# Carrying the odd layer's recurrence inside its chunk stage, with arrays turned in the features stage

## Chip, cores and metric

One core of a Trainium2 chip. The metric is device time in microseconds of one execution of the whole kernel, as the median over runs. "The profiled execution" is one further execution with the hardware profiler.

## What is computed

The kernel runs two transformer blocks over 512 latent and 256 context tokens, width 1024, all in float32. The first block has an attention layer and then an odd layer. One half of the odd layer's mixer is a gated delta rule (RWKV-7), run forwards and backwards for eight heads of 64, first over the context tokens and then, from the state left there, over the latent ones:

```python
def step(S, inp):
    w_t, k_t, v_t, kk_t, a_t = inp[:5]
    sa = jnp.einsum('bhvk,bhk->bhv', S, kk_t)
    S = (S * w_t[:, :, None, :] - sa[..., None] * (kk_t * a_t)[:, :, None, :]
         + v_t[..., None] * k_t[:, :, None, :])
    return S, (jnp.einsum('bhvk,bhk->bhv', S, inp[5]) if emit else None)
```

The outputs y of both directions over the latent tokens are needed, and of the context only the final state.

## The kernel before

Every part is a stage of its own: `stage` (L31) opens a block in which each engine runs its own instruction list, ordered by semaphores alone, and ends with a barrier over all engines. Engines are named PE (TensorE), DVE (VectorE), ACT (ScalarE), POOL (GpSimd) and SP (SyncE, which here only issues DMAs). `steps_of` (L91) unrolls two steps and runs the rest as a loop of two. The 768 tokens (context first) are cut into NCH = 12 chunks of CH = 64; CC = 4 of them are context. Three stages carry the recurrence.

**rwkv_features (L1431)** loops over four tiles m of 128 feature rows by 768 tokens. SP loads r, k, v and small weights of tile m, and the modulation weights of a later layer (`wbuf`, 3 MB twice per tile), which `modulate` multiplies beside (L1546). PE makes the gate products X and Y (L1558, L1561) for both directions, the head norms Z (L1566), the output gate (L1570) and the bonus sum (L1576). ACT takes sigmoids, square root and exponents, DVE the scan of the decays (L1605), the reciprocal (L1596) and the products alpha, beta, kappa, rho (L1624 to L1627). POOL stores those feature-major to `rwkv_arrays`. Tile m+1 starts when the bonus of m (`tail_ready`) is done.

**rwkv_chunks (L1668)** treats each chunk by itself, both directions d at once. SP's `load` (L1731) brings nine tiles with feature rows on the partitions; load(i) waits until chunk i-2 has ended, and PE reads them at the start of chunk i. PE multiplies in 64x64 corners, `each` (L1758) being eight products for the four head pairs (16 records in the trace). One chunk is: keys with alpha and rho (`kar`), turns of beta and kappa, betas with alpha and rho (`bar`), turns of alpha, v and z, masks times v (`mv`), five levels of doubling in which z and x are updated (lx by PE, copied by ACT, then two products each for x and z, added by DVE), then au and the results g, f, h, y. DVE masks the results of `kar` and `bar`; POOL makes the level masks `lev` (L1940) and stores the four results to `rwkv_ch` (L1947).

**rwkv_recurrence (L1955)** reads these back and carries the state over the 12 chunks: state = (g . state + h) * w, y = state . f + y, with four rounds PE to DVE per chunk, and stores ys. The readout stage follows. Another scan, **gla_chunks (L2257)**, in the second block, is not changed; it carries its state inside its chunk loop and loads with `kqr` tiles of 64 partitions and `vf` tiles of 128.

## Time and profile before

| | us |
|---|---|
| runs | 5564.84, 5576.18, 5569.65 |
| median | 5569.65 |
| profiled execution | 5565.43 |
| its span, first to last instruction | 5563.8 |
| TensorE / VectorE / ScalarE busy | 4503.7 / 2522.7 / 1470.3 |

The views group instructions by source line, engine and tile: output tile, an arrow, input tiles. In a timeline "x16" is how many records were merged, and the bracket is the engine's idle time ahead with what ended it; "issue" there is idle time that no wait of the profile explains, or a wait on a semaphore that it does not show. TensorE's clock has two levels, 1.2 GHz (0.50) and 2.4 GHz (1.00); a granted clock between them is a mean over both. One matmul in float32 is two records.

### The profile page before, as it was taken

To read this page: it belongs to the slowest core of one execution; us is meant where nothing else is said; L and a number is where in the kernel's file an instruction comes from. 1 tells how busy PE (TensorE), PEld (TensorE's weight loads), DVE (VectorE), ACT (ScalarE), POOL (GpSimd) and SP (SyncE) were. 2 spreads that over 40 slices of the span, in tenths; PEclk is the share of its full clock that TensorE was granted. 3 is DMA by queue.
4 is the path that set the end of the run, shared out by engine and by line. 5 is a ranking of instruction groups with operands and counts; after the bars stand their busy time and mean duration, and the time that the engine had idled before them with its cause. 6 is when DMAs were issued, how large, how long until landed. Compare 5 with 4: busy or idle time off the path is not lost. (4 is left out here: it accounts for less than half of the span.)

```text
span 5563.8 us, 87721 instructions
## 1 busy us (share of the span) xinstructions
PE 4503.7 (81%) x35800; PEld 3791.5 (68%) x35800; DVE 2522.7 (45%) x3576; ACT 1470.3 (26%) x2457; POOL 585.6 (11%) x789
## 2 busy tenths in 40 slices
PE   7567799999885587757996949389999995656998
PEld 7444588888742477745995838278888883435997
DVE  3454443336356444435444232343335845764444
ACT  2144321123243111102222221222213322333222
POOL 2011100001011211211001000010001112320000
PEclk7788899999996799978998955599999996668999
DMA  3355322213467312143332322222222333342332
GB/s 126 100 174 174 127 63 67 65 57 92 132 218 261 107 51 57 53 138 104 93 94 64 100 82 55 75 95 69 59 65 65 106 117 119 117 155 81 96 95 72
DMA packets 671562, 561.57 MB, mean 101 GB/s; under 512 B 114269, under 2 KB 582433, under 8 KB 671232
## 3 DMA queue, kind: packets, MB, share of 16 engines
q1 hardware_dynamic: 639552, 453.54, 27.1%
q0 software_dynamic: 31680, 103.21, 5.1%
q8 instruction: 258, 4.23, 0.3%
q14 instruction: 72, 0.59, 0.0%
HBM read 459.96 MB, written 96.69 MB: 100 GB/s over the span
## 5 line engine op out<-in xcount | busy, mean ns | idle before, releaser
L86 PE MATMUL acc<-h_hi,w_hi 128*128 128x258 f32 (+2 forms) x4416 | 1402.3, 318 | 45.8 <-DVE h_lo L455 39.2
L88 PE MATMUL acc<-h_hi,w_lo 128*128 128x258 f32 (+2 forms) x4416 | 1398.7, 317 | 0.0
L87 PE MATMUL acc<-h_lo,w_hi 128*128 128x258 f32 (+2 forms) x4416 | 1397.2, 316 | 0.0
L86 PEld LDWEIGHTS acc<-h_hi,w_hi 128*128 128x128 f32 x4416 | 833.0, 189 | 113.1 <-DVE h_lo L455 22.8
L87 PEld LDWEIGHTS acc<-h_lo,w_hi 128*128 128x128 f32 x4416 | 833.9, 189 | 60.5 <-issue 0.5
L88 PEld LDWEIGHTS acc<-h_hi,w_lo 128*128 128x128 f32 x4416 | 833.4, 189 | 59.0
L334 ACT CAST w_hi<-staged 128x1024 fp32r<-128x1024 f32 (+1 forms) x414 | 406.9, 1028 | 576.2 <-PE acc L88 391.0
L442 DVE TENSOR_TENSOR w_lo<-staged,w_hi 128x1024 fp32r<-128x1024 f32 (+1 forms) x414 | 480.5, 1200 | 139.8 <-ACT w_hi L334 137.0
L86 PE MATMUL acc<-hidden_hi,w_hi 128*128 128x512 f32 (+1 forms) x1200 | 419.3, 349 | 66.9 <-DVE hidden_lo L573 66.9
L483 DVE COPY offset<-acc 128x2 f32<-128x2 f32 x276 | 43.7, 158 | 928.9 <-PE acc L88 926.1
L87 PE MATMUL acc<-hidden_lo,w_hi 128*128 128x512 f32 (+1 forms) x1200 | 418.9, 349 | 0.0
L88 PE MATMUL acc<-hidden_hi,w_lo 128*128 128x512 f32 (+1 forms) x1200 | 418.0, 348 | 0.0
L86 PEld LDWEIGHTS acc<-hidden_hi,w_hi 128*128 128x128 f32 x1200 | 228.8, 191 | 98.1 <-issue 68.8
L88 PEld LDWEIGHTS acc<-hidden_hi,w_lo 128*128 128x128 f32 x1200 | 228.5, 190 | 29.2
L87 PEld LDWEIGHTS acc<-hidden_lo,w_hi 128*128 128x128 f32 x1200 | 228.7, 191 | 28.5
L598 POOL COPY squares<-square 128x768 f32<-128x768 f32 (+1 forms) x8 | 6.4, 797 | 1717.8 <-ACT square L345 1717.8
L494 DVE SCALAR_TENSOR_TENSOR xT<-acc,modTsecond,xT 128x512 f32<-128x512 f32 x104 | 66.6, 666 | 256.6 <-PE acc L88 256.6
L388 ACT CAST hidden_hi<-up 128x768 f32 (+3 forms) x66 | 50.4, 763 | 487.3 <-DVE up L513 487.3
L2783 PEld LDWEIGHTS diag_ps<-xd,decay 128*128 128x128 f32 x512 | 94.6, 284 | 107.7 <-DVE decay L2907 107.6
L494 DVE SCALAR_TENSOR_TENSOR xT<-acc,modTfirst,xT 128x512 f32<-128x512 f32 x96 | 60.5, 658 | 233.3 <-PE acc L88 233.2
L384 ACT ACTIVATE gate<-gate,offset 128x512 f32<-128x512 f32 (+1 forms) x132 | 81.3, 647 | 319.7 <-DVE gate L484 319.7
L1160 PE MATMUL raw<-k_hi,q 128*128 128x512 f32 (+3 forms) x240 | 90.4, 382 | 88.6 <-DVE q L1255 85.4
(451 smaller groups left out, 7045.2 us busy)
## 6 DMA issues: line engine op xcount, KB each, us to landing
wmod<-in_mod_w SPq DMA_DIRECT2D x16, 3072.0 KB, 14.8
staged<-in_w_ffn_in SPq DMA_DIRECT2D x88, 512.0 KB, 4.6
staged<-in_ffn_w_in SPq DMA_DIRECT2D x88, 512.0 KB, 4.4
wmod<-in_w_mod SPq DMA_DIRECT2D x8, 3072.0 KB, 11.0
rows<-acum SPq DMA_DIRECT2D x48, 512.0 KB, 3.8
staged<-in_ssd_w_in SPq DMA_DIRECT2D x42, 512.0 KB, 4.6
wmod<-in_w_mod SPq DMA_DIRECT2D x8, 2048.0 KB, 8.2
proj<-gate POOLq DMA_DIRECT2D x40, 384.0 KB, 2.6
```

The lines of the kernel that those rows point to most:

```text
L86: nc.tensor.matmul(out, w[0], x[0], start=start, stop=False)
L87: nc.tensor.matmul(out, w[0], x[1], start=False, stop=False)
L88: return nc.tensor.matmul(out, w[1], x[0], start=False, stop=stop)
L334: nc.scalar.copy(ws[s].hi[:, 0:p.KT, cols], staged[:, 0:p.KT, cols]).then_inc(S["w_hi"], 1)
L384: op = nc.scalar.activation(gate[s][:, t0:t0 + tn], gate[s][:, t0:t0 + tn], ACT.Silu, bias=offset[s][0][:, b:b + 1])
L388: nc.scalar.copy(hidden.hi[:, bass.ds(i, 1), 0:TOK - lo], up[s][:, wide]).then_inc(S["hidden_hi"], 1)
L442: nc.vector.tensor_tensor(ws[s].lo[:, 0:p.KT, cols], staged[:, 0:p.KT, cols], ws[s].hi[:, 0:p.KT, cols].bitcast(F32), ALU.subtract).then_i ...
L483: nc.vector.tensor_copy(offset[s][j][:], a[:, 254:256])
L494: op = nc.vector.scalar_tensor_tensor(out=xt, in0=acc[2 * s + j][:, c0:c0 + tn], scalar=p.gates[:, bass.ds(2 * i + j, 1), b], in1=xt, op0= ...
L598: op = nc.gpsimd.tensor_copy(squares[:, wide], square[j][:, wide])
L1160: nc.tensor.matmul(b[:, c:c + size], q2[s][:, t.q0:t.q0 + P], k_hi[g % 2][:, key:key + size], start=True, stop=False)
L2783: mm = nc.tensor.matmul(diag_ps[d][:, h], decay[d][:, h], xd[d][:, h], start=True, stop=True)
```

## The change

The recurrence stage and the array `rwkv_ch` are gone. The chunk stage walks each direction in its own order (`order`), loads both feature-major and token-major arrays (24 DMAs per chunk, 8 of 128 partitions and 16 of 64), and carries the state in SBUF: per chunk two products with the state per direction (context chunks one), accumulated into the open sums. Context chunks leave out what only y needs. The part of the next chunk that needs no state, its "front" (kar, bar, the masks, the turn of z), is placed into the current chunk: one product set after the lx sets of each of levels 0 to 3, and the turn behind au. Level 4 leaves out the x product. PSUM gets two banks `front`; most SBUF tiles are doubled.

The features stage is written out over its four tiles. It turns alpha, beta, kappa of both directions and v into token-major form: `flip` on PE makes six 128x128 transposes into Z, `take` on ACT copies Z to one of two buffers, POOL stores it. Norms of tile m+1 are made within tile m, each direction has its own tiles, the gate copy moves to ACT, the scaling of lw goes into the exponents' scale, and the modulation weights come in four parts per tile.

```diff
-def rwkv_features(nc, mixed, w2, a2, g2, cols, block_ones, reset_table, arrays, dec, bonus, gate, beside):
+def rwkv_features(nc, ident, mixed, w2, a2, g2, cols, block_ones, reset_table, arrays, by_token, v_by_token, dec, bonus, gate, beside):
...
+                def load(m):
+                    s, cut = m % 2, slice(m * P, m * P + P)
+                    after(sp, tail_ready, m - 1)
+                    for n, t in ((1, k[s]), (0, r[s]), (2, v[s])):
+                        sp.dma_start(t[:], mixed[m * P + n * RW:m * P + n * RW + P, :]).then_inc(loaded[s], 16)
...
+                def norms(m):
+                    pe.wait_ge(kk_squared, m + 1)
+                    after(pe, taken, 7 * m - 3)
+                    for t0, tn in parts:
+                        mm = nc.tensor.matmul(Z[:, t0:t0 + tn], block_ones[:], sq[:, t0:t0 + tn], start=True, stop=True)
+                    mm.then_inc(kk_summed, 1)
+                def flip(u, src):
+                    after(pe, taken, u)
+                    for t in range(TOK // P):
+                        tr = nc.tensor.transpose(Z[:, t * P:(t + 1) * P], src[:, t * P:(t + 1) * P], ident[:])
+                    tr.then_inc(turned, 1)
...
+                norms(0)
...
+                for m in range(TILES):
+                    gates(m, 0)
+                    pe.wait_ge(kk_root, m + 1)
+                    flip(7 * m, v[m % 2])
+                    gates(m, 1)
                     pe.wait_ge(sig_ready, 2 * m + 2)
                     for t0, tn in parts:
+                        mm = nc.tensor.matmul(Y[:, t0:t0 + tn], gs[m % 2][:], sg[:, t0:t0 + tn], start=True, stop=True)
                     mm.then_inc(gate_ready, 1)
+                    for j in range(UNITS // 2):
+                        modulate(UNITS * m + j)
+                    pe.wait_ge(four[0], m + 1)
+                    for n, t in enumerate((alpha[0], beta[0], kappa[0])):
+                        flip(7 * m + 1 + n, t)
+                    if m + 1 < TILES:
+                        norms(m + 1)
+                    for j in range(UNITS // 2, UNITS):
+                        modulate(UNITS * m + j)
...
+                    pe.wait_ge(four[1], m + 1)
+                    if m + 1 < TILES:
+                        pe.wait_ge(kk_root, m + 2)
+                    for n, t in enumerate((alpha[1], beta[1], kappa[1])):
+                        flip(7 * m + 4 + n, t)
...
+                def take(u, sign):
+                    act.wait_ge(turned, u + 1)
+                    after(act, flip_stored[u % 2], 16 * (u // 2))
+                    nc.scalar.mul(flipped[u % 2][:], Z[:, 0:TOK], sign).then_inc(taken, 1)
...
+                for m in range(TILES):
+                    sigmoids(m, 0)
+                    sigmoids(m, 1)
+                    take(7 * m, 1.0)
+                    exponents(m, 0)
+                    exponents(m, 1)
+                    act.wait_ge(gate_ready, m + 1)
+                    after(act, tail_stored, 32 * m)
+                    nc.scalar.copy(gat[:], Y[:, 0:TOK]).then_inc(gate_taken, 1)
+                    for n, sign in enumerate((1.0, -1.0, 1.0)):
+                        take(7 * m + 1 + n, sign)
+                    if m + 1 < TILES:
+                        squares(m + 1)
+                        root(m + 1)
+                    for n, sign in enumerate((1.0, -1.0, 1.0)):
+                        take(7 * m + 4 + n, sign)
...
+                    if m + 1 < TILES:
+                        keys(m + 1)
+                    for d in range(2):
+                        dve.wait_ge(exps[d], m + 1)
+                        dve.wait_ge(bonus_in, m + 1)
+                        V.tensor_tensor(alpha[d][:], kk[s][:], alpha[d][:], ALU.mult)
+                        V.tensor_tensor(beta[d][:], beta[d][:], down[d][:], ALU.mult)
+                        V.tensor_tensor(kappa[d][:], kappa[d][:], down[d][:], ALU.mult)
+                        V.tensor_tensor(rho[d][:], r[s][:], rho[d][:], ALU.mult).then_inc(four[d], 1)
...
+                def store_flipped(u, dst, m):
+                    pool.wait_ge(taken, u + 1)
+                    pool.dma_start(dst.rearrange("(t p) f -> p t f", p=P)[:, :, m * P:(m + 1) * P], flipped[u % 2][:]
+                                   ).then_inc(flip_stored[u % 2], 16)
...
+                for m in range(TILES):
+                    store_flipped(7 * m, v_by_token, m)
+                    store(m, 0)
+                    for n in range(3):
+                        store_flipped(7 * m + 1 + n, by_token[0, n], m)
+                    store(m, 1)
+                    for j in range(UNITS):
+                        store_mod(UNITS * m + j)
...
+                    for n in range(3):
+                        store_flipped(7 * m + 4 + n, by_token[1, n], m)
...
+def rwkv_chunks(nc, ident, masks_table, arrays, by_token, v_by_token, dec, ys):
...
+            def chunks(eng, body):
+                for i in range(CC + 2):
+                    body(i, i % 2, i >= CC, i + 1 >= CC)
+                with eng.Fori(CC // 2 + 1, NCH // 2 - 1) as t:
+                    for s in range(2):
+                        body(2 * t + s, s, True, True)
+                for i in range(NCH - 2, NCH):
+                    body(i, i % 2, True, True)
...
+                def half(t, c):
+                    return t.rearrange("t (h c f) -> c t h f", c=2, f=HD)[c]
+                def load(i, s, latent):
+                    if not (type(i) is int and i < 2):
+                        sp.wait_ge(S["core_p"], 2 * i - 2)
...
+                        cols = bass.ds(order(i, d, latent) * CH, CH)
+                        for dst, n in ((ka[s][d][:], 2), (ar[s][d][:, :, 0, :], 0), (be[s][d][:], 1), (ar[s][d][:, :, 1, :], 3)):
+                            sp.dma_start(dst, arrays[d, n].rearrange("(h k) t -> k h t", k=P)[:, :, cols]).then_inc(loaded[s], 16)
+                        for c in range(2):
+                            for dst, src in ((vt[s][d], v_by_token), (am[s][d][:, :, 0, :], by_token[d, 0]),
+                                             (bq[s][d][:, :, 0, :], by_token[d, 1]), (kt[s][d], by_token[d, 2])):
+                                sp.dma_start(dst[corners[c]], half(src[cols, :], c)).then_inc(loaded[s], 16)
...
+                load(0, 0, False)
...
+                for i in range(1, CC):
+                    load(i, i % 2, False)
+                with sp.Fori(CC // 2, NCH // 2) as t:
+                    for s in range(2):
+                        load(2 * t + s, s, True)
+            def arrived(eng, i, s):
+                eng.wait_ge(loaded[s], (i - s) * 192 + 384)
...
+                def keys_with(i, s, d, latent):
+                    arrived(pe, i, s)
+                    if latent:
+                        each(pair(front[d]), ka[s][d], pair(ar[s][d]), "kar")
+                    else:
+                        each(front[d][:, :, 0, :], ka[s][d], ar[s][d][:, :, 0, :], "kar")
...
+                def turn(i, s, d):
+                    wait(pe, "z1", i, d)
+                    apart()
+                    for h in range(H):
+                        for c in corners:
+                            tr = nc.tensor.matmul(front[d][c, h, 0, :], z[s][d][c, h], ident[c, c], start=True, stop=True)
+                    tr.then_inc(S["x1_t"], 1)
...
+                def core(i, s, latent, next_latent):
...
+                        if latent and not (type(i) is int and i <= CC):
+                            pe.wait_ge(S["y_c"], 2 * i + (d - 1 - 2 * CC))
+                        each(six[d], mp[s][d][:, :, 0, :], vt[s][d], "mv_p")
                     for n in range(LEV):
                         for d in range(2):
                             if n == 0:
                                 wait(pe, "x1", i, d)
+                                wait(pe, "levels", i, d)
+                                if not fresh(i):
+                                    wait_last(pe, "state_c", i, d)
                             else:
+                                wait(pe, "x_c", i, d, n - 1, LEV - 1)
                                 wait(pe, "z_c", i, d, n - 1, LEV)
+                            each(one[d], lev[s][d][n], x[s][d], "lx_p")
+                        if ahead and n < 4:
+                            (keys_with, keys_with, betas_with, betas_with)[n](i + 1, s1, n % 2, next_latent)
                         for d in range(2):
                             if n == 0:
                                 wait(pe, "mv_c", i, d)
                             wait(pe, "lx_c", i, d, n, LEV)
+                            if n < LEV - 1:
+                                each(six[d], z[s][d], lx[d], "x_p")
+                            each(one[d], lx[d], z[s][d], "z_p")
                     for d in range(2):
                         wait(pe, "z_c", i, d, LEV - 1, LEV)
+                        each(pair(big[d]), z[s][d], pair(am[s][d]), "au_p")
+                    for d in range(2):
+                        each(one[d], kt[s][d], vt[s][d], None, stop=False)
+                        if latent:
+                            each(six[d], vt[s][d], mp[s][d][:, :, 1, :], None, stop=False)
+                    if ahead:
+                        for d in range(2):
+                            turn(i + 1, s1, d)
                     for d in range(2):
...
+                        if latent:
+                            each(pair(big[d]), au[d][:, :, 0, :], pair(bq[s][d]), "gf_p")
+                        else:
+                            each(big[d][:, :, 0, :], au[d][:, :, 0, :], bq[s][d][:, :, 0, :], "gf_p")
+                    for d in range(2):
+                        each(one[d], bq[s][d][:, :, 0, :], au[d][:, :, 1, :], None, start=False, stop=False)
+                        if latent:
+                            each(six[d], au[d][:, :, 1, :], bq[s][d][:, :, 1, :], None, start=False, stop=False)
+                    for d in range(2):
+                        wait(pe, "gf_c", i, d)
+                        if fresh(i):
+                            pe.wait_ge(S["cleared"], 2)
+                        each(one[d], grow[d], state[d], None if latent else "core_p", start=False)
+                        if latent:
+                            each(six[d], state[d], read[d], "core_p", start=False)
...
+                def mask_betas(i, s, d, latent):
+                    wait(dve, "bar", i, d)
+                    V.tensor_copy(lt[s][d][:], front[d][:, :, 0, :]).then_inc(S["lt_ready"], 1)
+                    if latent:
+                        V.tensor_tensor(bq[s][d][:, :, 1, :], front[d][:, :, 1, :], wide(masks[:, d, 2, :]), ALU.mult)
+                    wait(dve, "lt_ready", i, d)
+                    V.tensor_tensor(z[s][d][:], lt[s][d][:], wide(masks[:, d, 3, :]), ALU.mult).then_inc(S["z1a"], 1)
+                    wait(dve, "z1a", i, d)
+                    V.tensor_tensor(z[s][d][:], z[s][d][:], wide(eye), ALU.add).then_inc(S["z1"], 1)
...
+                            V.tensor_tensor(z[s][d][:], z[s][d][:], one[d][:], ALU.add).then_inc(S["z_c"], 1)
+                        if ahead and n < 4:
+                            (mask_keys, mask_keys, mask_betas, mask_betas)[n](i + 1, s1, n % 2, next_latent)
...
+                    if ahead:
+                        for d in range(2):
+                            first_x(i + 1, s1, d)
```

## Rows read from the trace of the kernel before

**Rows 1.** busy time by stage (us, PE, PEld, DVE, ACT, POOL busy, clock, DMA share, GB/s)
```profile
1664.00:1878.00 214.00, 100.44 (x624) 49.46 (x624) 131.04 (x148) 58.78 (x71) 42.48 (x80) 0.60 0.60 219
1878.00:2403.00 525.00, 409.71 (x11136) 392.78 (x11136) 224.09 (x480) 98.63 (x264) 104.49 (x144) 0.96 0.21 55
2403.00:2480.00 77.00, 37.42 (x768) 35.79 (x768) 28.57 (x75) 0.00 (x0) 11.98 (x16) 0.70 0.58 192
```

**Rows 2.** timeline of TensorE, chunk stage (start us, us, engine, line, op)
```profile
1945.37 1.44 PE L1762 MATMUL one<-x,lev 64*64 64x64 f32 x32
1946.62 0.66 PE L1762 MATMUL six<-lx,z 64*64 64x64 f32 x16
1947.08 0.66 PE L1762 MATMUL one<-z,lx 64*64 64x64 f32 x16
...
1953.79 0.33 PE L1762 MATMUL one<-z,lx 64*64 64x64 f32 x2 [1.47 <-issue]
...
1969.20 1.07 PE L1762 MATMUL big<-bq,au 64*64 64x128 f32 x16
1970.07 0.31 PE L1835 MATMUL six<-mp,vt 64*64 64x64 f32 x4
```

**Rows 3.** what SyncE's queue waited for, chunk stage (us in total, times, longest)
```profile
SPq L1734 <- DVE res L1894: 344.2, 10, 39.4
```

**Rows 4.** timeline of SyncE's queue in the next scan, gla_chunks
```profile
3293.44 1.94 SPq L2305 DMA_DIRECT2D kqr<-gla_arrays  x3
...
3411.07 2.20 SPq L2305 DMA_DIRECT2D kqr<-gla_arrays  x3
...
3416.59 0.44 SPq L2307 DMA_DIRECT2D vf<-proj  x1
```

**Rows 5.** DMA issues of gla_chunks: KB each, median us to landing
```profile
kqr<-gla_arrays SPq DMA_DIRECT2D x72, 64.0 KB, 2.4
```

**Rows 6.** timeline of TensorE across one turn of the chunk loop
```profile
2313.09 3.67 PE L1762 MATMUL big<-ar,ka 64*64 64x128 f32 x32 [4.58 <-issue]
...
2355.21 1.94 PE L1762 MATMUL big<-ar,ka 64*64 64x128 f32 x32
```

**Rows 7.** costliest groups of VectorE, chunk stage (busy, mean ns | idle before)
```profile
L1867 DVE TENSOR_TENSOR z<-z,masks 128x256 f32<-128x256 f32 x24 | 19.9, 831 | 0.8
```

**Rows 8.** timeline of TensorE, features stage
```profile
1773.30 1.52 PE L1558 MATMUL X<-tanh_w,w 64*128 64x512 f32 x4 [1.21 <-DVE bon L1641]
...
1825.58 2.93 PE L1566 MATMUL Z<-sq,block_ones 128*128 128x512 f32 x4
...
1841.74 6.44 PE L1546 MATMUL mod_ps<-wmod,condsecond 128*32 128x192 f32 x128
```

**Rows 9.** groups of VectorE, features stage
```profile
L1596 DVE RECIPROCAL nrm<-nrm 128x768 f32<-128x768 f32 x4 | 19.8, 4953 | 0.1
L1605 DVE TENSOR_TENSOR_SCAN c<-reset,lw 128x768 f32<-128x768 f32 x8 | 14.1, 1758 | 0.3
L1627 DVE TENSOR_TENSOR o<-r,exp_c 128x768 f32<-128x768 f32 x8 | 7.7, 959 | 0.3
```

**Rows 10.** groups of ScalarE, features stage
```profile
L1518 ACT ACT_TABLE_LOAD x4 | 5.1, 1283 | 0.1
...
L1518 ACT ACTIVATE nrm<-Z 128x768 f32<-128x768 f32 x4 | 3.2, 811 | 18.3 <-PE Z L1566 18.3
```

**Rows 11.** timeline of TensorE, transposes of the attention stage
```profile
335.59 0.87 PE L1170 MATMUL probsT_ps<-ident,probs 128*128 128x128 f32 x6
336.22 0.47 PE L1160 MATMUL raw<-k_hi,q 128*128 128x512 f32 x1
```

**Rows 12.** DMA issues of the features stage
```profile
rwkv_arrays<-o POOLq DMA_DIRECT2D x32, 384.0 KB, 5.8
```

**Rows 13.** busy time, clock and DMA rate in two stretches (columns as Rows 1)
```profile
1884.00:1888.00 4.00, 0.19 (x2) 0.22 (x4) 0.00 (x0) 0.00 (x0) 0.00 (x0) 0.50 1.29 219
3300.00:3500.00 200.00, 192.07 (x960) 166.91 (x960) 40.76 (x73) 31.62 (x72) 17.95 (x24) 0.50 0.22 53
```

724 lines of the change are left out of this document (273 added, 451 removed).

## The prediction

> **What bounds the kernel now.** I read the busy time by stage first [rows 1]. The change touches three stages in a row: features (214 us), chunks (525 us) and recurrence (77 us), 816 of the 5563.8 us of the span. Stages end in a barrier over all engines, so their times add up. In the chunk stage TensorE is busy 410 of 525 us at a clock of 0.96, so this stage is TensorE's own instruction stream plus some waits. In the other two no engine is full and the clock is 0.60 and 0.70: these are chains of waits.
>
> The timeline of TensorE then gives two prices in the chunk stage [rows 2]. One product set of one direction (16 records, 64 columns) starts the next after 0.46 us (1946.62 to 1947.08), called u; a 128-column set takes 0.87 us (1969.20 to 1970.07), called w. In a level, the sets that need lx start 1.25 us after the first lx set, 0.3 us more than two sets take. There are also pauses that no engine explains (1.47 us at 1953.79); I count about 1.8 us of such pauses in a chunk.
>
> The third view is what SyncE's queue waited for [rows 3]: ten loads waited 344.2 us in sum for the end of an earlier chunk, up to 39.4 us each. So the queue was idle most of the time, and its nine loads had a whole chunk (525 / 12, about 43 us) before TensorE needed them. This is cover that the change uses up.
>
> **The change, part by part: chunk stage.** Per direction, a latent chunk now takes four w sets and 22 u sets (the turns of beta, kappa, alpha and v and one x product are gone; two state products are new): 13.6 us, 27.2 for both. A context chunk takes one w and 22 u, 22.0 us. Before, it was four w and 25 u, 30 us. So TensorE's work falls by 12 x 30 = 360 to about 306 us, and the 77 us of the recurrence stage go.
>
> What is added: load(i) has 24 DMAs instead of nine. It still waits until chunk i-2 has ended, but its first reader, keys_with(i), now stands in chunk i-1 behind mv and the lx sets of level 0, about 2 us after that end. The load is therefore on the path, in every chunk from the third. Its price: in gla_chunks eight such issues take 3411.07 to 3417.03, 5.96 us, 0.745 each inside a loop, and 1.94 / 3 = 0.65 each unrolled [rows 4]; the last lands 2.4 us after its issue [rows 5]. Load = 24 x 0.745 + 2.4 + 0.3 for the semaphore = 20.6 us in the loop (chunks 4 to 11), 18.2 unrolled (chunks 0 to 3). Lower bound: the bytes, 24 DMAs are 2.1 MB, at the 219 GB/s that 256-byte runs reached [rows 13] are 9.6 us, with landing 12.3. Upper bound: 24, if stores of ys get in between. I take the issue-bound value, since those rows have the same size and shape as 16 of the 24.
>
> The Trainium skill, DMA: Bandwidth & Descriptors, section Anatomy of one DMA, fits one DMA (issued by GpSimd) as 2.0 us plus bytes / 436e3 in us. Taken for all 2.1 MB in one, that is 6.8 us (an estimate from that page) and would take nearly 14 us off each chunk; the 0.745 us issue pitch of the trace speaks against using it here, and it is not in the sum.
>
> From keys_with on, a latent chunk costs 27.2 - 4 u = 25.4 us of sets, 0.3 for level 4 (in the others the front covers the lx copy), 1.8 of pauses, and two more. First, VectorE now has mask_betas between levels: four operations of at most 0.83 us [rows 7], I take 2.5 us, after levels 2 and 3 where TensorE's next result waits behind them; late by about 1.5 us in a chunk (0 to 4). Second, after the wait for the load TensorE is cold: the first set pair after an idle 4.58 us took 3.67 us against 1.94 in the running loop [rows 6], and with the work behind it I take 2.5 us (1.7 to 5). Sum 31.5; context chunks 20.2 + 0.3 + 1.3 + 0.8 + 2.5 = 25.1. GpSimd's level masks run two levels ahead of their reader and are free. The state product and its scaling lie beside the other direction's sets: nothing, and 0.5 us a chunk if that cover goes.
>
> Path from the first issue: load(0), three small issues and load(1) end at 35.5 us (front(0) hides in it); chunk 0 ends at 60.6. Chunks 1 and 2: 18.2 + 25.1 each, 147.2. Chunk 3 with a latent front: 20.6 + 27.4, 195.2. Chunks 4 to 10: 7 x (20.6 + 31.5) = 364.7, 559.9. Chunk 11 has no load and no front: 26, 586. Copy, store and barrier 6: 592. Against 525 + 77 = 602 this is -10 us. The loop turn of 4.58 us [rows 6] falls into the load's time.
>
> **Features stage.** The turns move here: per tile of 128 rows seven arrays, each as six transposes into Z, then a ScalarE copy out of Z. There is one Z, so transposes and copies alternate. Six transposes in the warm clock take 2 x 0.63 = 1.26 us [rows 11], cold twice that. The copy is like nrm<-Z, 0.81 us [rows 10], 0.9 with hand-over. The X, Y and Z products of 768 columns take 1.5 warm and 2.9 cold [rows 8]. One tile, from its first gate product, cold / warm:
> gates 0: 5.8 / 3.0, the v turn, gates 1 and sigmoid: 15.0 / 8.2. VectorE: scan and two passes 3.7 (1.76, 0.96 [rows 9]), ten passes 8.5, four products 3.9: 31.1 / 24.3. Three turns 10.2 / 6.5: 41.3 / 30.8. Squares 0.9 and norms 2.9 / 1.5: 45.1 / 33.2. Two mod units (half of 6.44 us, rows 8 has the four): 48.3 / 36.4. Bonus: 51.2 / 37.9. Three turns without the last copy: 60.5 / 43.5, and only then the next tile's gates.
> The reciprocal (4.95 [rows 9]) and norms now lie in the shadow of the tile before, which is the gain in it; exponent waits on the stores go too. Before, a tile takes (1773.30 - 1664 - 11) / 2 = 49 us. The stage's clock of 0.60 [rows 1] is one fifth warm; with denser work I take one third warm: 60.5 - 5.7 = 55. Start: loads and keys 12, squares, norms, root 4.6, then Tanh and Sigmoid with a table load of 1.28 each [rows 10], 21 in all. Stage: 21 + 4 x 55 - 3.5 (no norms in the last) = 237.5, last copy and GpSimd's backlog 3, landing 5.8 [rows 12], barrier 5: 251 against 214, +37 (bounds -9 all warm, +59 all cold). GpSimd's queue has the mod stores ahead of the second direction's turned arrays; that delays the third copy some 2 us per tile, hidden behind the next gates.
>
> **Sum.** +37 - 10 = +27: 5565.4 (the profiled execution) + 27 = 5592 us. The median of the three runs, 5569.65, lies 0.08% above that execution.
>
> **Rivals.** (A) The forecast: both added chains show, 5592; own range 5560 to 5640. Chance 0.62.
> (B) Faster: the load does not cost its issues. Place: the wait of TensorE ahead of keys_with. If it comes down to the 12.3 us of its bytes, eight loads save 8.3 and two 5.9 each, 78 us, and the time is 5514; with warm features 5468. It decides from about 17.9 us of load in the loop (27 us over ten loads). For it: 219 GB/s [rows 13]. Against it: 0.745 us per issue with a DMA share of only 0.22 in that stage [rows 4, 13], so the issues were not held up by the engines. Chance 0.20. The skill's fit named above (DMA: Bandwidth & Descriptors) points the same way as B.
> (C) Much slower: with a wait in every chunk TensorE's clock stays low. gla_chunks shows it: 192 of 200 us busy and clock 0.50 throughout [rows 13], and the features stage is mostly low. Price: 0.87 more per unit of set time, 25.4 x 0.87 - 2.5 = 20 us for eight latent chunks and 15 for four context ones, +220: 5810. Against it: the same 64*64 sets on both corners ran at 0.96 [rows 1] and recovered after 4.58 us idle [rows 6]. Chance 0.07.
> (D) No change within 0.2%: features come out at 50 us per tile (+17) beside the chunk stage as summed (-10): 5572. Chance 0.11.
>
> **How the numbers follow.** About 0.2% (11 us) is what a measurement of this kernel can tell from no change. B goes to faster with 0.19, C and nearly all of A to slower, D and the edges of A and B to same: 0.19, 0.13, 0.68. The range reaches into B down to 5520 (half of B is below) and up over A's edge to 5660, where load 24, VectorE 4 and cold features would meet; 0.1 is left below and 0.1 above (C and the rest).
>
> **What would show it.** In the changed profile: at keys_with, TensorE idle about 18 us in each chunk, put down to a DMA, with SyncE's 24 issues in a row ahead of it; chunk period near 52 us latent and 43 context; first sets after it at twice their time; no recurrence stage; features with a period near 55 and copies flipped<-Z in threes with transposes in between, 3 us apart. Wrong would be: TensorE not idle at keys_with, an issue pitch near 0.4 us, a tile period under 49, or a chunk-stage clock near 0.5.

## The result, and the profile after

The changed kernel took 5591.3 us (median of five runs, 5590.8 to 5599.8) against 5567.7 us for the kernel before (5564.8 to 5576.2): a ratio of 1.0045, 95% interval 1.003 to 1.006. It is slower by some 24 us, where 5592 was predicted. The profiled execution has a span of 5589.6 us.

The busy time by stage comes first, as in [rows 1]. The limits of a stage are SyncE's first issue in it and its first issue in the next one.

```profile
core 0: us, PE busy (x) PEld busy (x) DVE busy (x) ACT busy (x) POOL busy (x), PEclk, DMA share, GB/s
1663.15:1923.56 260.41, 130.11 (x1304) 83.32 (x1304) 117.20 (x124) 82.69 (x103) 81.59 (x140) 0.64 0.63 222
1923.56:2508.37 584.81, 361.91 (x9600) 349.19 (x9600) 202.88 (x442) 59.61 (x160) 104.48 (x136) 0.82 0.22 50
```

By the same limits the kernel before had 214.4 us of features and 601.4 us of chunks and recurrence together. So features grew by 46.0 us, the chunk stage gained 16.6 against the two stages that it replaces, readout took 1.3 more and the rest of the program 4.9 less (it is the same code): 46.0 - 16.6 + 1.3 - 4.9 = 25.8 us, which is the difference of the two spans. The total was met; its two terms had been put at +37 and -10.

**The chunk stage.** This is TensorE's timeline across one latent chunk, from the last sets of one chunk to the last of the next:

```profile
2126.40 1.13 PE L1848 MATMUL one<-x,lev 64*64 64x64 f32 x32
2143.48 1.97 PE L1848 MATMUL front<-ar,ka 64*64 64x128 f32 x16 [15.95 <-DMA kt<-rwkv_turned]
2145.21 1.09 PE L1848 MATMUL six<-lx,z 64*64 64x64 f32 x16
...
2148.67 1.47 PE L1848 MATMUL one<-x,lev 64*64 64x64 f32 x32
...
2150.86 0.63 PE L1848 MATMUL six<-lx,z 64*64 64x64 f32 x16
2151.32 0.63 PE L1848 MATMUL one<-z,lx 64*64 64x64 f32 x16
...
2177.49 1.13 PE L1848 MATMUL one<-x,lev 64*64 64x64 f32 x32
```

and SyncE's queue in the same stretch (first and last issues of one load, first of the next):

```profile
2125.83 0.38 SPq L1819 DMA_DIRECT2D ka<-rwkv_arrays  x1
...
2141.15 0.54 SPq L1823 DMA_DIRECT2D kt<-rwkv_turned  x1
2176.69 0.38 SPq L1819 DMA_DIRECT2D ka<-rwkv_arrays  x1
```

TensorE stands still for 15.95 us at keys_with, put down to the last DMA of the load, and starts 17.65 us after SyncE's first issue: 15.3 us until the 24th issue begins (0.67 each) and 2.3 until it has landed. From there to the next load's first issue (2143.48 to 2176.69) a latent chunk takes 33.2 us; the period is 50.9. The set behind the wait runs at half speed: ka and the four sets of level 0 take 5.19 us (2143.48 to 2148.67), later sets follow at 0.46 us again (2150.86 to 2151.32), as u in [rows 2]. The same pattern stood in the kernel before at the turn of the loop alone [rows 6]. Over the stage this is one group of the list of costliest groups:

```profile
L1848 PE MATMUL front<-ar,ka 64*64 64x128 f32 (+1 forms) x384 | 31.6, 323 | 198.5 <-DMA kt<-rwkv_turned 198.5
...
L1848 PE MATMUL front<-ar,be 64*64 64x128 f32 (+1 forms) x384 | 23.0, 260 | 1.9 <-DVE mp L1953 1.9
```

198.5 us of waiting for the load in twelve waits: 36.8 us before the first chunk, 4.1 for the load of the second, then ten of 12.0 to 17.0 us, nine of them near 16.

**The features stage.** Here are ScalarE and GpSimd at the turn from the first tile to the second (GpSimd's rows are DMA issues):

```profile
1730.59 0.81 ACT L1594 ACTIVATE flipped<-Z 128x768 f32<-128x768 f32 x1 [4.69 <-PE Z L1521]
1732.37 0.81 ACT L1594 ACTIVATE flipped<-Z 128x768 f32<-128x768 f32 x1 [0.96 <-PE Z L1521]
1746.22 0.81 ACT L1594 ACTIVATE flipped<-Z 128x768 f32<-128x768 f32 x1 [13.05 <-DMA rwkv_turned<-flipped]
1747.05 1.28 ACT L1599 ACT_TABLE_LOAD   x1
```

```profile
1731.97 4.18 POOL L1712 DMA_DIRECT2D mod_rowssecond<-mod_row  x8 [2.82 <-DVE mod_row L1688]
1736.14 0.57 POOL L1725 DMA_DIRECT2D bonus<-bon  x1
1736.70 0.56 POOL L1726 DMA_DIRECT2D gate<-gat  x1
1737.25 1.67 POOL L1699 DMA_DIRECT2D rwkv_turned<-flipped  x2
1747.33 0.83 POOL L1699 DMA_DIRECT2D rwkv_turned<-flipped  x1 [8.41 <-ACT flipped L1594]
```

The third copy of the three of direction 1 stands still for 13.05 us. It reuses the buffer of the first of them, and that one, copied at 1730.59, is only issued for store at 1737.25, behind eight issues of modulation rows and the tile's two tail stores; then it takes until 1746 to land. (In the stage the median from issue to landing is 3.9 us for this kind; for the three in this stretch it is 8.9.) The next tile's Sigmoid of X, whose product TensorE finished at 1735.6, stands behind that copy in ScalarE's order and starts at 1748.35. The waits of ScalarE and VectorE in the stage (engine, what waits, for what: us in total, times, longest):

```profile
ACT flipped L1594 <- DMA rwkv_turned<-flipped: 59.6, 8, 13.8
```

```profile
DVE mod_row L1688 <- DMA mod_rowssecond<-mod_row: 64.2, 8, 16.5
```

### The profile page after: what moved, and what is told of

Read it like the earlier page. It is cut to its first block and busy times, and to the rows that moved or that the text cites. A ratio compares the mean times of both kernels' runs of the same rounds, so it can differ in the third digit from the quotient of the medians.

```text
span 5589.6 us, 83951 instructions
## 1 busy us (share of the span) xinstructions
PE 4447.0 (80%) x34176; PEld 3748.8 (67%) x34176; DVE 2460.3 (44%) x3440; ACT 1455.1 (26%) x2385; POOL 612.9 (11%) x825
## 5 line engine op out<-in xcount | busy, mean ns | idle before, releaser
L1848 PE MATMUL front<-ar,ka 64*64 64x128 f32 (+1 forms) x384 | 31.6, 323 | 198.5 <-DMA kt<-rwkv_turned 198.5
## 6 DMA issues: line engine op xcount, KB each, us to landing
wmod<-in_mod_w SPq DMA_DIRECT2D x16, 1536.0 KB, 10.1
```

Of the source, the lines that this page charges most:

```text
L1848: mm = nc.tensor.matmul(out[c, h], lhs[c, h], rhs[c, h], start=start and (stop or h == 0), stop=stop and (start or h == H - 1))
```

## The experiments

Two theories follow from this profile. T1: in the chunk stage a load costs its 24 issues on one queue, and all of that is exposed at keys_with. T2: in the features stage it is the third copy's wait for a late store that lengthens the tile, not the alternation of transposes and copies through Z, which the prediction had priced. All lengths of stages, here and in the tables, are read as above.

### The key arrays first

```diff
-                        for dst, n in ((ka[s][d][:], 2), (ar[s][d][:, :, 0, :], 0), (be[s][d][:], 1), (ar[s][d][:, :, 1, :], 3)):
...
+                    for d in range(2):
+                        for dst, n in ((ka[s][d][:], 2), (ar[s][d][:, :, 0, :], 0), (ar[s][d][:, :, 1, :], 3)):
+                            whole(dst, d, n, f"keys{s}{d}")
+                    for d in range(2):
+                        whole(be[s][d][:], d, 1, f"betas{s}")
...
                 def keys_with(i, s, d, latent):
-                    arrived(pe, i, s)
+                    pe.wait_ge(S[f"keys{s}{d}"], (i - s) * 24 + 48)
...
                 def betas_with(i, s, d, latent):
                     wait(pe, "mp_ready", i, d)
+                    pe.wait_ge(S[f"betas{s}"], (i - s) * 16 + 32)
...
                 def core(i, s, latent, next_latent):
                     ahead, s1 = has_next(i), 1 - s
+                    arrived(pe, i, s)
```

(whole issues one full array and counts it on the semaphore named; the sixteen halves follow, on loaded[s])

> The changed kernel with one thing altered: in the chunk stage a load's key arrays (ka and both halves of ar of direction 0, then of direction 1, then both be) are issued first on semaphores of their own, and the sixteen halves of the token-major arrays last; keys_with waits for three DMAs, betas_with for two more, and the product of mp and vt for the rest. Theory (the load is exposed because TensorE waits for all 24 issues): the first keys_with can run 3 x 0.6 + 2.4 + 0.3 = 4.5 us after the chunk before has ended, against 18.1 us now; TensorE's level-0 sets take 2.3 us of that, so its idle time there falls from 16.0 us to about 2.5 us, ten times: the chunk stage goes from 585 us to about 450 us (latent period from 51 us to about 37 us), the whole to about 5455 us. Rival R1 (the sixteen late DMAs are then waited for by the next reader, or their traffic slows it): part of the wait comes back at the product of mp and vt, gain under 60 us. Rival R2 (TensorE's clock, now 0.81 in the stage, is set by the stage's own pattern and not by the waits): gain 135 us from the idle time alone with the clock unchanged; with the waits gone the theory has it rise to 0.95 or more, as before the change.

Measured: 5457.3 us, ratio to the kernel before 0.9811 (0.9795 to 0.9828). The chunk stage took 444.4 us instead of 584.8. TensorE's groups and one chunk of its timeline:

```profile
L1855 PE MATMUL front<-ar,ka 64*64 64x128 f32 (+1 forms) x384 | 28.0, 292 | 50.1 <-DMA ar<-rwkv_arrays 49.2 <-issue 0.8
...
L1855 PE MATMUL front<-ar,be 64*64 64x128 f32 (+1 forms) x384 | 23.1, 260 | 13.4 <-DVE mp L1962 13.4
```

```profile
2155.29 1.09 PE L1855 MATMUL front<-ar,ka 64*64 64x128 f32 x16 [2.29 <-DMA ar<-rwkv_arrays]
...
2158.05 1.44 PE L1855 MATMUL one<-x,lev 64*64 64x64 f32 x32
```

The wait at keys_with fell to 2.3 us; the same five sets (ka and level 0) now take 2.76 us, so 2.4 us of the 5.19 above was the half-speed clock after the long wait. The clock of the stage rose from 0.82 to 0.92. This chunk is one of the good ones, though. In five of the ten chunks the first set still runs at half speed, among them the chunk just before, behind a wait of the same length:

```profile
2119.71 1.97 PE L1855 MATMUL front<-ar,ka 64*64 64x128 f32 x16 [2.29 <-DMA ar<-rwkv_arrays]
```

So the slow start became rarer and shorter, but did not go; no run shows what decides it. R1 is out: the sixteen late DMAs are waited for nowhere (no row of TensorE names them). R2 is out as well, though the clock stopped short of the 0.95 that the theory gave. The 13.4 us ahead of betas_with are a single wait before the first chunk: VectorE starts only when the table of masks and the decays are there (19.7 us, put down to the decays' load), and these loads stand behind the 24 DMAs of load(0). It was there before, hidden in the wait for that load.

### The issues on two queues, and eight more of them

```diff
-                    for d in range(2):
+                    for d in range(1):
...
                     if has_next(i):
                         levels(i + 1, 1 - s)
+                    if not (type(i) is int and i >= NCH - 2):
+                        load(i + 2, s, not (type(i) is int and i + 2 < CC))
```

(the second hunk is in GpSimd's core; its load issues the twelve DMAs of d = 1 on semaphores of their own)

> The changed kernel with the loads of direction 1 in the chunk stage (12 of the 24 DMAs of each chunk) issued by GpSimd instead of SyncE; TensorE still waits for all 24 at the first keys_with. Theory (the load costs its issues on one queue, 24 x 0.65 to 0.72, plus 2.4 landing): each queue issues 12, so a load takes 12 x 0.7 + 2.7 = 11 us, TensorE's idle time at keys_with falls from 16.0 us to 9 to 10 us, the chunk stage by 60 to 70 us to about 520 us. Rival (the load costs its bytes: 2.1 MB in 256-byte runs at about 219 GB/s is 9.6 us plus landing, and the engines are near that already): idle stays at 13 us or more, gain at most 30 us.

Measured: 5535.6 us in one run, chunk stage 530.9 us. SyncE's first issue of a load, GpSimd's last, and TensorE's first set:

```profile
2151.07 0.39 SPq L1819 DMA_DIRECT2D ka<-rwkv_arrays  x1
...
2158.26 0.54 SPq L1823 DMA_DIRECT2D kt<-rwkv_turned  x1
```

```profile
2158.77 0.62 POOL L2065 DMA_DIRECT2D kt<-rwkv_turned  x1
```

```profile
2163.90 1.97 PE L1849 MATMUL front<-ar,ka 64*64 64x128 f32 x16 [10.91 <-DMA kt<-rwkv_turned]
```

The last issue begins after 7.7 us instead of 15.3, and the load takes 12.8 us instead of 17.65: of the 7.6 us of issuing that were taken away, 4.8 were gained. The last transfer now lands 5.1 us after its issue began instead of 2.3. One could put that down to GpSimd's queue itself, but SyncE's own issues land later too. This is the median from issue to landing in the chunk stage (1970 us to its end), first in the changed kernel, then here:

```profile
kt<-rwkv_turned SPq DMA_DIRECT2D x40, 64.0 KB, 2.3
```

```profile
kt<-rwkv_turned SPq DMA_DIRECT2D x20, 64.0 KB, 5.3
kt<-rwkv_turned POOLq DMA_DIRECT2D x20, 64.0 KB, 5.0
```

The DMA engines are busy 0.96 of the time from 2151 to 2164, against 0.53 during the load of the changed kernel (2126 to 2143.5). So both sides hold a part: on one queue the issues set the pace, on two the transfer begins to show. The idle time, expected at 9 to 10 us, was 10.9.

```diff
+        spare = [[sb(f"spare{s}{n}", [16, CH]) for n in range(8)] for s in range(2)]
...
+                    for n in range(8):
+                        sp.dma_start(spare[s][n][:], arrays[0, 1, 16 * n:16 * n + 16, 0:CH]).then_inc(loaded[s], 16)
```

> The changed kernel with eight more DMAs behind the 24 of each load, each of 16 rows of 64 numbers (4 KB) into tiles that nothing reads, waited for with the others. Theory (a load costs its issues on SyncE): 8 x 0.56 to 0.72 = 4.5 to 5.8 us more per load, TensorE idle at keys_with 21 us instead of 16, chunk stage longer by 45 to 60 us (ten exposed loads and the first two). Rival (a load costs its bytes; 32 KB more of 2.1 MB are nothing): idle time and stage unchanged within 5 us.

```profile
2154.05 3.83 SPq L1826 DMA_DIRECT2D spare<-rwkv_arrays  x8
```

```profile
2159.30 1.97 PE L1851 MATMUL front<-ar,ka 64*64 64x128 f32 x16 [19.91 <-DMA spare<-rwkv_arrays]
...
2213.50 1.97 PE L1851 MATMUL front<-ar,ka 64*64 64x128 f32 x16 [19.45 <-DMA spare<-rwkv_arrays]
```

The chunk stage took 627.1 us, 42.3 more, and the wait in a latent chunk grew from 16.0 us to 19.5 and 19.9. 32 KB of data cost 3.5 to 3.9 us per load: eight issues of 0.48 us. The rival is out; the 45 to 60 us expected were a little too much, since these small issues take 0.48 us each and not 0.56 or more.

### The front one level later

```diff
-                        if ahead and n < 4:
-                            (keys_with, keys_with, betas_with, betas_with)[n](i + 1, s1, n % 2, next_latent)
+                        if ahead and n > 0:
+                            (keys_with, keys_with, betas_with, betas_with)[n - 1](i + 1, s1, (n - 1) % 2, next_latent)
```

(and the masks on VectorE likewise)

> The changed kernel with the next chunk's front placed one level later: keys_with behind the lx sets of levels 1 and 2, betas_with behind those of levels 3 and 4 (and the masks on VectorE one level later as well). Theory (the load's end is fixed by the end of the chunk before, and whatever TensorE does ahead of keys_with hides it): one more level, 3.5 to 4 us in the clock after a wait, lies in the cover; TensorE's idle time falls from 16.0 us to about 12 us, the stage by about 35 to 40 us to 548 us; VectorE's last mask_betas (three operations, 1.8 us) then runs into level 4 and may give back 1 us a chunk. Rival (TensorE's sets are done in either order and the wait moves with them, because the transposes of z and the next x wait for the late masks): gain under 15 us, with a new idle time ahead of the transposes out of z.

Measured: 5544.9 us in one run, chunk stage 536.2 us, 48.6 less, where 35 to 40 were expected. TensorE waited 154.5 us in sum at keys_with, 44.0 less (9.6 to 13.5 us at the four waits from 2060 to 2250, where 12 were expected):

```profile
L1848 PE MATMUL front<-ar,ka 64*64 64x128 f32 (+1 forms) x384 | 31.2, 319 | 154.5 <-DMA kt<-rwkv_turned 154.5
L1848 PE MATMUL big<-am,z 64*64 64x128 f32 x384 | 23.6, 271 | 1.8 <-DVE z L1984 1.1
```

The place of keys_with decides how much of the load is covered, and VectorE's masks give nothing back: the wait ahead of the products with am, 6.1 us in the changed kernel, is 1.8 here.

### Four buffers for the turned tile

```diff
-        flipped = [sb(f"flipped{u}", [P, TOK // P, P]) for u in range(2)]
+        flipped = [sb(f"flipped{u}", [P, TOK // P, P]) for u in range(4)]
...
-                    after(act, flip_stored[u % 2], 16 * (u // 2))
-                    nc.scalar.mul(flipped[u % 2][:], Z[:, 0:TOK], sign).then_inc(taken, 1)
+                    after(act, flip_stored[u % 4], 16 * (u // 4))
+                    nc.scalar.mul(flipped[u % 4][:], Z[:, 0:TOK], sign).then_inc(taken, 1)
```

> The changed kernel with four buffers (and four semaphores) for the turned tile in the features stage instead of two, so that ScalarE's copy out of Z waits for the store before the fourth last one. Theory (the last of three copies in each direction waits for a store that GpSimd issues late, behind the mod rows, and that lands 8 us later; the copies stand in ScalarE's order ahead of the next tile's sigmoids): the 13 to 14 us that ScalarE was idle ahead of the sixth copy of a tile and the 3 us ahead of the third go; the tile period falls from 59.8 us to about 45 us, the features stage from 260 us to 200 to 210 us. Rival R1 (the alternation of TensorE and ScalarE through the single Z is what costs, as the prediction had it): the copies move earlier but the period stays at 55 us or more, gain under 20 us. Rival R2 (the modulation weights, 3072 rows of each tile loaded beside it, bound the stage once the copies are free): the period stops near 50 us with TensorE waiting for wmod.

Measured: 5565.2 us, ratio to the kernel before 0.9999 (0.9988 to 1.001). The features stage fell from 260.4 to 227.1 us and the period of the second tile from 59.8 to 46.3 (a period is the time from VectorE's product bon, the end of a tile, to that of the next).

```profile
1726.77 0.81 ACT L1594 ACTIVATE flipped<-Z 128x768 f32<-128x768 f32 x1 [4.11 <-PE Z L1521]
1728.54 0.81 ACT L1594 ACTIVATE flipped<-Z 128x768 f32<-128x768 f32 x1 [0.96 <-PE Z L1521]
1730.32 0.81 ACT L1594 ACTIVATE flipped<-Z 128x768 f32<-128x768 f32 x1 [0.96 <-PE Z L1521]
...
1733.14 0.90 ACT L1599 ACTIVATE lw<-X,packed 128x768 f32<-128x768 f32 x1
```

```profile
DVE mod_row L1688 <- DMA mod_rowssecond<-mod_row: 62.5, 8, 16.4
```

```profile
PE mod_ps L1546 <- DMA wmod<-in_mod_w: 17.5, 5, 6.0
...
PE Z L1521 <- ACT flipped L1594: 14.4, 16, 0.9
```

The three copies follow each other at 1.78 us, the next tile's Sigmoid starts at 1733.14, and ScalarE waits for no store. T2 holds, R1 is out: TensorE waits 14.4 us in the whole stage for copies out of Z. The chunk stage, which is the same code, took 586.2 us. The gain of 33 us is less than the 50 to 60 that were expected, and there are two candidates for what ends the tile now: VectorE waits 62.5 us for stores of modulation rows, TensorE 17.5 us for the weights.

### What ends the tile then

First the key arrays and the four buffers together, then these with the front one level later.

> The changed kernel with key arrays first and with four buffers for the turned tile, both as in the runs before. Theory (two separate chains in two stages that a barrier divides): the gains add up, 135 + 27 us below the changed kernel, features 227 us and chunks 444 us: 5428 us, 2.5% below the kernel before the change. Rival (one gain hides in the other, through the clock or through DMA traffic): less than 150 us in sum.

> Key arrays first, four buffers for the turned tile, and the front one level later. Theory (2.3 us of waiting are left ahead of the first keys_with in each chunk, 1 us ahead of betas_with for VectorE's masks): one level of cover takes both away, 2.5 to 3.5 us in each of ten chunks: chunk stage about 415 us, the time about 5398 us. Rival (VectorE's last masks now run into the end of the chunk, where the copies of au wait behind them): the gain is half or less, or nothing.

Then variants of the features stage. Without turning, flip and take only pass their semaphores on, and the stores write zeros, so that the scan works on zeros in the place of the turned arrays:

```diff
                 def flip(u, src):
...
-                    tr.then_inc(turned, 1)
+                    pe.sem_inc(turned, 1)
...
                 def take(u, sign):
                     act.wait_ge(turned, u + 1)
-                    after(act, flip_stored[u % 2], 16 * (u // 2))
-                    nc.scalar.mul(flipped[u % 2][:], Z[:, 0:TOK], sign).then_inc(taken, 1)
+                    act.sem_inc(taken, 1)
```

> The changed kernel with the turning left out of the features stage: TensorE transposes nothing, ScalarE copies nothing, and GpSimd stores tiles of zeros in the place of the turned ones at the same points of its queue (so the token-major arrays hold zeros, and the scan's output is not the reference's). Against the run with four buffers (features 227 us, tile period 46.3 us) it gives the price of the transposes and copies themselves. Theory (the wait for stores was 13 us of the 59.8 us tile, and what is left of the turning, two groups of three turns of 5.3 to 6.4 us and one of v, lies partly beside the modulation weights): period 37 to 41 us, features 195 to 210 us. Rival R1 (the alternation through the single Z costs as much as the prediction had it, 17 us cold per tile): period 30 us, features below 180 us. Rival R2 (the weights and the other transfers bound a tile): period stays at 44 us or more, features 220 us or more.

Four row buffers, on top of the best version and later on the changed kernel alone:

```diff
-        mod_row = [sb(f"mod_row{j}", [P, MG]) for j in range(2)]
+        mod_row = [sb(f"mod_row{j}", [P, MG]) for j in range(4)]
...
-                        after(dve, mod_stored[u % 2], 16 * MOD_GROUPS * (u // 2))
+                        after(dve, mod_stored[u % 4], 16 * MOD_GROUPS * (u // 4))
```

> The version with key arrays first, four buffers for the turned tile and the front one level later, and now four small row buffers (with four semaphores) for the modulation rows in the features stage instead of two. Theory (with the turning out of the way a tile of 46 us ends when VectorE has copied the third and fourth row block, and those copies wait 14 to 18 us for the store of the first, whose issues stand in GpSimd's queue behind ten stores of the four products and three turned ones): the 59 us that VectorE waited for these stores in the run before go, the copies run when TensorE has summed them, about 6 us earlier per tile; period 40 us, features from 228 to about 203 us, time 5388 - 25 = 5363 us. Rival (the transfers bound the tile, the DMA engines being busy 0.72 of this stage: the modulation weights arrive no earlier): period at least 44.5 us, gain under 6 us, with TensorE waiting for wmod.

```diff
                 for m in range(TILES):
-                    if m + 1 < TILES:
-                        load(m + 1)
                     for j in range(UNITS):
+                        if m + 1 < TILES and j == (2 if m else 0):
+                            load(m + 1)
```

> As the one before, and in SyncE's queue of the features stage the first two of a tile's four loads of modulation weights stand ahead of the next tile's six loads, which wait for the end of the tile before. Theory (weights are asked for too late because their issues stand behind that wait): TensorE's waits for wmod (17.5 us in the run with four buffers) shrink by half, features 5 to 10 us shorter than without this. Rival (the weights' transfer time bounds, and the next tile's own arrays now come later): no gain, or up to 5 us longer.

> The changed kernel with the four small row buffers alone (the turned tile has two buffers as in the change, keys not first). Theory (the sixth copy of a tile waits for the store of the fourth, which GpSimd issues behind the third and fourth row block and the tail; with four row buffers these come about 3 us earlier, the rest of the store's way is the same): the tile period goes from 59.8 to about 56 us, features from 260 to 245 to 252 us, and ScalarE still waits 10 us or more ahead of the sixth copy. Rival (the row copies were the only limit and the wait of ScalarE merely followed them): features 215 us or less.

> The run without turning (zeros stored in the place of the turned arrays, so the scan's output is not the reference's), with the four small row buffers as well. Theory (the turning and the row stores are two chains of nearly equal length: with two row buffers a tile took 46 us with or without the turning, and with four row buffers but with the turning 48 us; taking both away leaves neither): the period falls to about 38 to 40 us and features to about 200 us, which makes the turning itself worth some 24 us of the stage once the stores no longer hold it. Rival (the transfers bound a tile at 46 us, since the stores of the turned arrays and the weights are the same here): features 218 us or more.

Measured (us; a ratio with its interval where there were several runs; "tiles" are the periods of the second, third and fourth tile):

```
                                time    ratio to before          features  chunks  tiles
kernel before                   5567.7                           214.4             49.3 46.9 44.1
changed kernel                  5591.3  1.0045 (1.003-1.006)     260.4     584.8   59.8 62.5 50.6
four buffers (above)            5565.2  0.9999 (0.9988-1.001)    227.1     586.2   46.3 48.9 47.1
both                            5414.7  0.9738 (0.9723-0.9753)   227.7     441.2   49.9 46.9 46.6
both, front later               5388.0  0.9693 (0.9677-0.9709)   228.2     413.5   45.8 51.5 46.9
both, later, four rows          5387.9  0.9683 (0.9670-0.9696)   224.2     424.6   48.6 44.0 44.4
the same, weights first         5384.9  0.9678 (0.9664-0.9691)   224.0     417.3   48.6 44.0 44.4
change with four rows alone     5577.7                           250.8     585.9   57.1 55.0 48.0
change without turning          5558.3                           225.7     581.8   46.0 51.7 45.8
the same with four rows         5534.3                           206.5     577.4   52.2 38.0 38.2
```

"Both" took off 176.7 us where 162 were expected. By stage it is 32.7 and 143.6 us, against 33.4 and 140.4 in the two runs apart, so the gains add up. (Each ratio is to the kernel before on the same chip, whose median lay between 5557.6 and 5567.7 us; times of different chips differ by as much.) With the front later the chunk stage lost another 28 us, as expected (415 us).

Two cautions for the features stage. Where its code is the same it took 256.0 to 260.4 us in five runs, so a difference of 4 us between single traces shows nothing. And one period says little, since they change from tile to tile; the sum of the three is steadier: 172.9 us in the changed kernel, 142.3 to 144.3 with four buffers.

Four rows alone gave 9.6 us and left ScalarE 48.4 us of waiting for stores instead of 59.6, up to 10.1 at a time, as expected. The others each missed in part. Taking the turning out entirely gave hardly more than the four buffers had (225.7 against 227.1), which looked like the transfers' bound; but the waits of VectorE in that run name the stores of the rows again:

```profile
DVE mod_row L1687 <- DMA mod_rowssecond<-mod_row: 56.1, 8, 17.9
```

Four rows on top of the best version took that wait away and still gained only 4 us of the stage (7 in the three periods, and 4 were lost behind the last one), so the row stores were not the only limit either. These are VectorE's waits in that run:

```profile
DVE mod_row L1688 <- issue: 24.3, 3, 9.7
...
DVE mod_row L1688 <- PE mod_ps L1546: 14.2, 5, 10.1
```

```profile
PE Z L1521 <- DVE rho L1683: 28.9, 4, 9.2
...
PE mod_ps L1546 <- DMA wmod<-in_mod_w: 5.5, 2, 3.4
```

VectorE now waits for TensorE's sums, which in TensorE's order stand behind the turns of direction 0 and the norms (for 14.2 us the row says so; the 24.3 us of "issue" stand at the same copies); TensorE waits for the weights in only two places, 5.5 us. The rival's gain for this run was right, its reason was not. Placing the weights first took away these waits of TensorE and changed nothing (224.0). Only without turning and with four rows did the stage fall, to 206.5. The last two of its tiles took 38 us each, as the theory had it. In that run the weights are late, and over those two tiles the DMA engines are busy 0.95 of the time at 339 GB/s (last two columns), against 0.71 and 247 GB/s in the changed kernel from 1732 to 1855:

```profile
PE mod_ps L1544 <- DMA wmod<-in_mod_w: 32.4, 7, 12.4
```

```profile
1776.00:1852.00 76.00, 48.97 (x564) 30.05 (x564) 58.05 (x62) 26.27 (x33) 35.24 (x59) 0.62 0.95 339
```

So behind the third copy's wait three limits seem to lie close together: the chain through the turns, the chain through GpSimd's row stores, and the transfers. With the first two away the stage is 206.5 us, against 224.2 with the turning in it. That the first two hold it together is shown by taking each away alone and both at once; that the transfers are what is left is argued from the rows above, and no run with fewer bytes tests it. Nor do the runs separate how the clock shares in this.

## Why the prediction was right, and where its steps were not

**The load on the path: right, its price 3 us too high.** Predicted was 20.6 us in the loop and 18.2 unrolled; from the first issue to TensorE's first set it was 17.65 and 17.5 (1985.84 to 2003.37). The term was the issue pitch of 0.745 [rows 4]: here the pitch was 0.67, since the full arrays are issued at 0.56 and only the halves at 0.72; that is 1.8 of the 3 us. The sum also counted 24 pitches where 23 lie between the first issue and the last. That it is the issues was shown from three sides: fewer per queue, more of them with hardly any bytes, and fewer ahead of the reader. On two queues the transfer showed too, and the load took 12.8 us, close to the lower bound of 12.3 that had been worked out from bytes. The Trainium skill, DMA: Bandwidth & Descriptors, section Anatomy of one DMA, would give 6.8 us for the bytes in one transfer (an estimate from that page); no run that waited for all 24 came below 12.8, so neither number of queues agrees with it as the price of such a load.

**The work from keys_with on: 31.5 predicted, 33.2 measured** in a latent chunk, 25.1 and 27.4 in a context chunk. The cold start was put at 2.5 us and was 2.4. The delay through VectorE's mask_betas was put at 1.5 us a chunk; TensorE's waits for VectorE's z ahead of the products with am come to 5.7 us in the whole stage, 0.7 at the longest. What was too low is the rest: the pauses of the chunk shown come to 2.6 us (0.54, 0.74 and 1.33) against 1.8, and two lx sets take 1.3 us there (2148.67 to 2149.99) and not 0.92; why they do stays open. Period 50.9 against 52.1, stage 584.8 against 592. The load saved 25 us over ten chunks and the work gave back 18. That put the load just below the 17.9 us from which rival B was to decide, and still the kernel was slower: the other terms of that threshold had moved against it.

**Features: +37 predicted, +46 measured, and by another cause.** The start was right (21 us; the first gate product at 1684.24 is 21.1 us in). The tile was put at 55 us by a chain in which transposes and copies through the single Z cost 10.2 us per direction when cold. Six transposes had been taken as 1.26 us warm and twice that cold; they took 0.87 and 1.54. The row of [rows 11] had been read as three transposes of two records each, but a transpose is one record: the six of `flip` are x6 in this trace too. The prediction had thus doubled their price, and three turns took 7.4 us cold and 5.2 in direction 1, where they run at the high clock behind the weights' products. And the norms, bonus and the next tile's gates lay beside other work: with the wait for the store gone a tile is 46 to 49 us, and even that ends on other stores. The step that failed is the last one of that part: "GpSimd's queue has the mod stores ahead of the second direction's turned arrays; that delays the third copy some 2 us per tile, hidden behind the next gates". The queue was seen, its price was not: the copy waited 13.1, 13.9 and 9.1 us at the three turns between tiles and was not hidden, because in ScalarE's order it stands ahead of the very sigmoids that were to hide it. Four buffers took 33 us of the 46 off again. A chain priced too high and a wait priced too low gave a tile of 55 where the periods were 59.8, 62.5 and 50.6. So the time was met partly by luck: features were 9 us above their price, the two stages of the scan 7 below theirs, and the wait had been put at nothing.

**The rivals.** C (the clock stays low) did not come: 0.82 over the stage, full speed after five sets. D needed features at 50 us a tile. B's mechanism is what the experiment with the key arrays makes of the change: with the load's late part hidden, the forecast for B (5514) is passed by 57 us, because nearly the whole wait goes and not only the issues' share.

The signs named ahead were found: the wait at keys_with (16 us; 18 expected), the 24 issues in a row, first sets at half speed, chunk periods of 50.9 latent and 45.0 context (52 and 43), copies in threes 1.8 to 2.4 us apart (3 expected), but the third of them 13 us late, which no sign had named.

The change itself was worth making: with both waits taken away and the front one level later the kernel runs in 5388 us, 3.1% below the kernel before. All of that is the chunk stage, carried recurrence included (601.4 to 413.5 us); the features stage is still 14 us longer than before.

## What to carry to other kernels

When a load moves onto the path, cut it by reader: issue first what the first reader needs, on a semaphore of its own, and let the rest land behind the work that doesn't need it. Here three of 24 DMAs were needed at once, and the order alone was worth 140 us of the stage. When a ring of two buffers is shared by more copies than it has places, look at what stands ahead of the store in the issuing queue and at what stands behind the waiting copy in its engine's order: here up to 13.9 us of waiting per tile, and 33 us of the stage for two more buffers. And a tile that ends on several chains of like length gives little for any one of them: with the ring's wait gone, 4 us for the row stores, 1 for the turning (neither is clear of what equal code varies by), and 21 for both.

## What was not expected of the hardware

A store's way from issue to landing was not a constant: 3.9 us in the median of the stage for the turned arrays, but 8.9 us for the three that were issued at 1737 to 1747, right behind SyncE's six loads and two weight tiles of 1.5 MB each. With two queues issuing at once the same halves of the chunk stage landed after 5.3 us instead of 2.3. In the chunk loop an issue on SyncE took 0.37 us and the next followed after 0.56 for an array over all 128 partitions, 0.54 and 0.72 for a half over 64 partitions; GpSimd, whose issues follow each other without a gap, needed 0.76 and 0.62 for the same two:

```profile
2106.02 0.76 POOL L2061 DMA_DIRECT2D ar<-rwkv_arrays  x1
...
2109.48 0.62 POOL L2065 DMA_DIRECT2D bq<-rwkv_turned  x1
```

So which of the two queues is the faster one depends on the shape of the transfer. And three runs whose chunk stage is the same code had 413.5, 424.6 and 417.3 us there, at clocks of 0.95, 0.93 and 0.94: a spread of 11 us that is no effect of the edit.
